# Column sums of squares in a two-block transformer kernel: from VectorE adds to accumulation in TensorE

## The chip, the cores and the metric

The kernel runs on one core of a Trainium2 chip. The metric is the device time of one execution in microseconds, the median of several runs. Inside the core, TensorE (PE) multiplies matrices and accumulates into PSUM, VectorE (DVE) and ScalarE (ACT) work element by element, GpSimd (POOL) does small jobs, and SyncE (SP) issues most of the DMA. Each engine runs its own queue in order, and the queues wait for each other on semaphores.

## What is computed

Two blocks on a sequence of 1024 tokens with 1024 features. The first has two layers, each an attention and a gated feed-forward network; the second is a mixer of a state-space model and short convolutions. Each stage begins with an RMS norm over the features:

```
def rmsnorm(x, g):
    y = x * lax.rsqrt(jnp.mean(x * x, axis=-1, keepdims=True) + RMS_EPS)
    return y * g

for i in range(DEPTH):                                   # first block, DEPTH = 2
    h = rmsnorm(x, norm_mix[i]) * (1 + sc1) + sh1        # norms 0 and 2
    x = x + g1 * attention_i(h)
    h = rmsnorm(x, norm_ffn[i]) * (1 + sc2) + sh2        # norms 1 and 3
    x = x + g2 * swiglu(h, ffn_w_in[i], ffn_w_out[i])
x = rmsnorm(x, final_norm)                               # folded with the next (4, 5)
... second block: rmsnorm, projections, scan, convolutions, out projection ...
return rmsnorm(h, final_norm_gain)                       # norm 6
```

The change concerns norms 1, 2, 3 and 6: norm 1 behind the first attention, norm 2 behind the first feed-forward stage, norm 3 behind the second attention, and norm 6 at the very end.

## The kernel before

The activations are held transposed: xT has 8 chunks (KC = 8) of 128 features on the partitions by 1024 tokens. A norm needs for each token the sum over all 1024 features. The kernel takes it in steps:

1. Each of the 8 chunks of the residual is finished by a VectorE add (L2337 behind attention, L2085 behind feed-forward, L2631 at the end). ScalarE squares it (L1565, at norm 6 L1900) into `squared(n, k)`.
2. VectorE adds the squares of chunks 1 to 7 into chunk 0 (`sum_squares`, L1966), one chunk behind the residual adds; the last add is in `deviations`.
3. TensorE multiplies the summed chunk by a column of ones (L1051): for each of 8 groups of 128 tokens the 128x128 square block is the stationary operand, and the moving operand has one column. The data are plain f32, and the trace has two instructions and two weight loads for each such matmul, so 16 of each for a chunk.
4. VectorE makes the variance (L1980), ScalarE its root (L1571), VectorE the reciprocal root (L1989 to L1993). TensorE spreads it over the partitions (L1059), and VectorE and ScalarE scale the chunks (L2022, L1579, L2018) for the next stage's matmuls. Norm 6 has no spread: TensorE transposes the result instead (L1541), and ScalarE and VectorE scale the transposed tiles (L1559, L2637) ahead of eight stores.

In TensorE's `norm(n)` the order is: 8 spare products into unused PSUM (L1044, they keep the engine working while it waits), the wait for the last VectorE sum, the narrow matmuls of step 3, 3 more spare products, the spread.

Behind the first feed-forward stage, TensorE makes the last down-projection in 8 tiles m = 0 to 7, six matmuls of 512 columns each (L1255). They go to four accumulators in PSUM in the order `LAST_PLACES = (2, 3, 0, 1, 2, 3, 2, 3)`; a tile whose place was used before waits until VectorE has added the earlier tile into xT (L2085). VectorE's loop there is `add_down(m)` and then `sum_squares(2, m - 1)`.

Which accumulator a step uses, and which counts of the semaphores it waits for, comes from a ledger (`plan_accumulators`), filled in program order.

Of the kernel before, what the change touches and what calls it, by code (L numbers as in the profile page):

```python
# [152 lines left out]
def plan_accumulators():  # L153
    use = Ledger()
    def norm(n):
        use.add(("norm sum", n), 3)
        use.add(("norm spread", n), 2, frees=0)

    for k in range(KC):
# [48 lines left out]
LAST_SPLITS = [name for name, _ in TILES if name[0] != "glu"]  # L208
MIX_TILES = [[(what, u) for u in us for what in ("kv", "q0", "q1")] for us in (range(4), range(4, 10))]
SPLITS = MIX_TILES[0] + [("wo", 0, m) for m in range(KC)] + MIX_TILES[1] + [("wo", 1, n) for n in range(4)] + LAST_SPLITS  # L210


def norm_turn(n):

    return min(n, 4) - 1
# [29 lines left out]
def two_blocks_kernel(nc, x, x_rows, c, ada_tiles, columns, ffn_w_in, ffn_w_out, a_tiles, a_w_out, a_sink,  # L245
# [6 lines left out]
    with ctx:  # L252
# [333 lines left out]
        def squared(n, k):  # L586

            return last_squares[k] if n == 6 else hT[:, k, :]
# [418 lines left out]
        def _(pe):  # L1007
# [38 lines left out]
            def norm(n):  # L1046
                dst, ready = take(("norm sum", n))
                spare_products(8, psum[:, 0:256] if n == 2 else psum[:, 3584:3840])
                pe.wait_ge(squares_summed, (KC - 1) * (norm_turn(n) + 1))
                for t in range(ST):  # L1050
                    mm = nc.tensor.matmul(dst[:, t:t + 1], squared(n, 0)[:, P * t:P * t + P], ones[:, :], start=True, stop=True)  # L1051
                mm.then_inc(ready, 1)
                if n == 6:
                    return
                dst, ready = take(("norm spread", n))
                spare_products(3)
                pe.wait_ge(rstd_ready, n + 1)
                for t in range(ST):
                    mm = nc.tensor.matmul(dst[:, P * t:P * t + P], rst[:, n, 4, t:t + 1].to_broadcast([P, P]), ident[:, :], start=True, stop=True)  # L1059
                mm.then_inc(ready, 1)  # L1060
                spare_products(8)
# [484 lines left out]
        def _(act):  # L1546
# [14 lines left out]
            def norm(n, wait_chunk, between=None):  # L1561
# [5 lines left out]
                        between(k)  # L1567
                if n == 2:
                    tile_highs(("q0", 4))
                act.wait_ge(acc_free[3], ACC[("norm sum", n)][2] + 1)  # L1570
                nc.scalar.activation(dev[:, n, :], var[:, n, :], ACT.Sqrt).then_inc(dev_ready, 1)  # L1571
                if n in (1, 3):
                    first_highs(n // 2)
# [337 lines left out]
        def _(dve):  # L1911
# [47 lines left out]

            def sum_squares(n, k):  # L1960

                if k > 0:
                    dve.wait_ge(squares, KC * norm_turn(n) + k + 1)
                    if (KC - 1) * norm_turn(n) + k > 1:
                        dve.wait_ge(squares_summed, (KC - 1) * norm_turn(n) + k - 1)
                    nc.vector.tensor_tensor(squared(n, 0), squared(n, 0), squared(n, k), ALU.add).then_inc(squares_summed, 1)  # L1966

            def norm(n):
# [6 lines left out]

            def deviations(n):

                sum_squares(n, KC - 1)
                a = ready(("norm sum", n))
                nc.vector.tensor_scalar(var[:, n, :], a[:, 0:ST], 1.0 / D, EPS, ALU.mult, ALU.add).then_inc(acc_free[3], 1)  # L1980
                dve.wait_ge(dev_ready, n + 1)
                reciprocal_root(n).then_inc(rstd_ready, 1)
                if n == 6:
                    dve.wait_ge(rstd_ready, 6)
# [53 lines left out]
            def feed(l, f):  # L2038
# [169 lines left out]
                for m in range(KC):  # L2208
                    add_down(STEPS - 1, m, acc[LAST_PLACES[m]])
                    if m == 0:  # L2210
                        down_lows(STEPS - 1, 1)
                    if l == 0:
                        sum_squares(2, m - 1)
                    if l == 1 and m == 1:
                        tile_lows(("conv", 0, 1))
                    if l == 1 and m >= 5:
                        gained_low(m - 5)
# [471 lines left out]
```

## Time and profile before

| | |
|---|---|
| median of 3 runs | 2823.31 us (2821.97 to 2825.81) |
| the profiled execution | 2823.84 us, span 2821.8 us |
| TensorE busy | 2692.6 us, 95% |
| VectorE busy | 1948.1 us, 69% |
| ScalarE busy | 1012.4 us, 36% |
| mean granted TensorE clock | 0.972 of full speed |

The span is from the first to the last instruction; the rest of the profiled execution's time lies around it. Busy shares are averages over stages. TensorE's clock has two levels, and the clock that the chip granted is given as a share of full speed: 1.00 is 2.4 GHz, 0.50 is 1.2 GHz. Weight loads (PEld) overlap with matmuls (PE).

### The profile page before, as it was taken

To read this page: it belongs to the slowest core of one execution; us is meant where nothing else is said; L and a number is where in the kernel's file an instruction comes from. 1 tells how busy PE (TensorE), PEld (TensorE's weight loads), DVE (VectorE), ACT (ScalarE), POOL (GpSimd) and SP (SyncE) were. 2 spreads that over 40 slices of the span, in tenths; PEclk is the share of its full clock that TensorE was granted. 3 is DMA by queue.
4 is the path that set the end of the run, shared out by engine and by line. 5 is a ranking of instruction groups with operands and counts; after the bars stand their busy time and mean duration, and the time that the engine had idled before them with its cause. 6 is when DMAs were issued, how large, how long until landed. Compare 5 with 4: busy or idle time off the path is not lost. (4 is left out here: it accounts for less than half of the span.)

```text
span 2821.8 us, 35472 instructions
## 1 busy us (share of the span) xinstructions
PE 2692.6 (95%) x12770; PEld 2120.5 (75%) x12770; DVE 1948.1 (69%) x3279; ACT 1012.4 (36%) x1789; POOL 271.9 (10%) x422
## 2 busy tenths in 40 slices
PE   6999699999999999999998989999999999999798
PEld 5666377788888888766675768888888878879767
DVE  6787747877778777667767597777777784331653
ACT  5554424333333332444444253333333341101232
POOL 2110000000000001101100000000000049920000
PEclk9999899999999999999998899999999999979899
DMA  5223321111111111223221111111111131121212
GB/s 225 98 98 101 138 90 53 49 52 50 55 51 52 56 48 49 97 68 98 91 82 75 34 38 57 51 56 52 48 56 52 49 113 38 45 46 32 82 38 75
DMA packets 172826, 193.08 MB, mean 68 GB/s; under 512 B 7952, under 2 KB 138224, under 8 KB 172432
## 3 DMA queue, kind: packets, MB, share of 16 engines
q1 hardware_dynamic: 160160, 147.45, 16.1%
q0 software_dynamic: 12560, 44.20, 5.1%
q8 instruction: 68, 1.11, 0.2%
q14 instruction: 38, 0.31, 0.0%
HBM read 177.86 MB, written 12.58 MB: 67 GB/s over the span
## 5 line engine op out<-in xcount | busy, mean ns | idle before, releaser
L2085 DVE SCALAR_TENSOR_TENSOR xT<-psum,mod,xT 128x1024 f32<-128x1024 f32 x352 | 446.6, 1280 | 143.0 <-PE psum L1255 143.0
L1255 PE MATMUL psum<-hT_high,w_low 128*128 128x512 f32 x1344 | 360.0, 390 | 4.1 <-DVE xT L2085 4.1
L1255 PEld LDWEIGHTS psum<-hT_high,w_low 128*128 128x128 f32 x1344 | 251.8, 188 | 58.6 <-DVE xT L2085 6.6
L1613 ACT ACTIVATE w_high<-wpair 128x512 fp32r<-128x512 f32 x294 | 184.6, 632 | 227.2 <-DMA wpair<-in_ffn_w_in_dram 129.4
L1036 PE MATMUL psum<-hT_high,w_low 128*128 128x512 f32 x944 | 260.2, 395 | 2.1 <-DVE arena L2481 2.1
L1036 PEld LDWEIGHTS psum<-hT_high,w_low 128*128 128x128 f32 x944 | 179.4, 191 | 40.5 <-DVE arena L2481 2.3
L1255 PE MATMUL psum<-h_low,w_low 128*128 128x512 f32 x672 | 207.6, 390 | 2.3 <-DVE h_low L2080 2.3
L1083 PE MATMUL psum<-hT_high,w_low 128*128 128x512 f32 x480 | 203.7, 424 | 1.9 <-DVE h_low_mix L2369 1.2
L1223 PE MATMUL psum<-hT_high,w_high 128*128 128x512 f32 x504 | 196.8, 391 | 3.5 <-DVE w_low L2045 3.5
L1732 ACT ACTIVATE arena<-arena 128x384 f32<-128x384 f32 (+3 forms) x320 | 157.7, 494 | 116.3 <-DVE arena L2266 116.3
L1224 PE MATMUL psum<-h_low,w_high 128*128 128x512 f32 x504 | 196.6, 390 | 0.0
L1225 PE MATMUL psum<-hT_high,w_low 128*128 128x512 f32 x504 | 196.4, 390 | 0.0
L1085 PE MATMUL psum<-hT_high,w_low 128*128 128x512 f32 x480 | 188.6, 393 | 0.0
L1084 PE MATMUL psum<-h_low_mix,w_low 128*128 128x512 f32 x480 | 187.8, 391 | 0.0
L2045 DVE TENSOR_TENSOR w_low<-wpair,w_high 128x512 fp32r<-128x512 f32 x252 | 172.8, 686 | 3.7
L2060 DVE TENSOR_TENSOR wpair<-wpair 128x512 f32<-128x512 f32 x168 | 115.9, 690 | 69.7 <-PE psum L1225 64.2
L1255 PEld LDWEIGHTS psum<-h_low,w_low 128*128 128x128 f32 x672 | 126.2, 188 | 29.2 <-DVE h_low L2080 3.1
L2351 DVE TENSOR_TENSOR w_low<-wpair,w_low 128x1024 fp32r<-128x1024 f32 x74 | 94.0, 1271 | 72.7 <-ACT w_low L1711 72.6
L1139 PE MATMUL psum<-arena 64*128 64x256 f32 (+3 forms) x640 | 119.8, 432 | 23.0 <-DVE arena L2260 20.8
L1083 PEld LDWEIGHTS psum<-hT_high,w_low 128*128 128x128 f32 x480 | 89.8, 187 | 64.0 <-issue 45.5
L1224 PE MATMUL psum<-hid_low,w_high 128*128 128x512 f32 x336 | 131.2, 391 | 0.0
L1631 ACT ACTIVATE hT<-hT 128x512 f32<-128x512 f32 x84 | 53.2, 633 | 168.3 <-DVE hT L2090 168.0
(340 smaller groups left out, 5261.1 us busy)
## 6 DMA issues: line engine op xcount, KB each, us to landing
wpair<-in_ffn_w_in_dram SPq DMA_DIRECT2D x176, 256.0 KB, 2.9
wpair<-in_ffn_w_out_dram SPq DMA_DIRECT2D x88, 256.0 KB, 2.8
wpair<-in_ada_tiles_dram POOLq DMA_DIRECT2D x20, 1024.0 KB, 5.4
wpair<-in_ada_tiles_dram POOLq DMA_DIRECT2D x32, 512.0 KB, 3.6
wpair<-in_w_in_dram SPq DMA_DIRECT2D x24, 512.0 KB, 3.8
wpair<-in_b_tiles_dram SPq DMA_DIRECT2D x18, 512.0 KB, 3.3
arena<-in_ada_tiles_dram SPq DMA_DIRECT2D x8, 1024.0 KB, 16.4
out_dram<-xT SPq DMA_DIRECT2D x16, 512.0 KB, 3.0
```

What stands on the lines that cost most here:

```text
L1036: mm = nc.tensor.matmul(dst[:, HALF * t:HALF * t + HALF], w(k), src(k)[:, HALF * t:HALF * t + HALF], start=first and n == 0 and w is high ...
L1083: nc.tensor.matmul(dst, high[:, k, :], hT_high[:, k, rows], start=k == 0, stop=False)
L1084: nc.tensor.matmul(dst, high[:, k, :], h_low_mix[:, k, rows], start=False, stop=False)
L1085: mm = nc.tensor.matmul(dst, low[:, k, :], hT_high[:, k, rows], start=False, stop=k == KC - 1)
L1223: nc.tensor.matmul(bank[dst], high[:, k, :], high_of(k), start=start and k == 0, stop=False, skip_group_check=not start)
L1224: nc.tensor.matmul(bank[dst], high[:, k, :], low_of(k), start=False, stop=False, skip_group_check=not start)
L1225: mm = nc.tensor.matmul(bank[dst], low[:, k, :], high_of(k), start=False, stop=k == 3, skip_group_check=not start)
L1255: mm = nc.tensor.matmul(dst[:, HALF * t:HALF * t + HALF], w, src[:, t, :], start=n == 0, stop=n == 2)
L1613: nc.scalar.activation(part_high[name], part_raw[name], ACT.Copy).then_inc(part_high_ready, 1)
L1732: e = nc.scalar.activation(s, s, ACT.Exp, bias=stat_n[:, ti, h:h + 1], accum_out=stat_l[:, ti, h:h + 1])
L2045: nc.vector.tensor_tensor(part_low[name], part_raw[name], as_f32(part_high[name]), ALU.subtract).then_inc(part_split, 1)
L2085: nc.vector.scalar_tensor_tensor(xT[:, m, :], acc[m % 2] if src is None else src, mod[:, l, 40 + m:41 + m], xT[:, m, :], ALU.mult, ALU.add ...
```

## The change

At norms 1, 3 and 6 VectorE still adds chunks 0 to 5, and TensorE accumulates this sum and the squares of chunks 6 and 7 as three series of narrow matmuls into the same eight PSUM columns. At norm 2 VectorE adds nothing; TensorE accumulates all eight chunks. The sum of norm 2 goes to accumulator 1 instead of 3, so it waits for the add of tile 3.

```
 def plan_accumulators():
     use = Ledger()
     def norm(n):
-        use.add(("norm sum", n), 3)
+        use.add(("norm sum", n), 1 if n == 2 else 3)
...
+SUMMED_ALONE = {1: (6, 7), 2: tuple(range(1, KC)), 3: (6, 7), 6: (6, 7)}
+SUMS = KC - 3
+
+def sums_before(n):
+    return SUMS * {1: 0, 2: 1, 3: 1, 6: 2}[n]
...
             def norm(n):                                       # TensorE
                 dst, ready = take(("norm sum", n))
                 spare_products(8, psum[:, 0:256] if n == 2 else psum[:, 3584:3840])
-                pe.wait_ge(squares_summed, (KC - 1) * (norm_turn(n) + 1))
-                for t in range(ST):
-                    mm = nc.tensor.matmul(dst[:, t:t + 1], squared(n, 0)[:, P * t:P * t + P], ones[:, :], start=True, stop=True)
+                if n != 2:
+                    pe.wait_ge(squares_summed, sums_before(n) + SUMS)
+                else:
+                    pe.wait_ge(down_added, KC * (STEPS - 1) + 4)
+                for k in (0,) + SUMMED_ALONE[n]:
+                    if k or n == 2:
+                        pe.wait_ge(squares, KC * norm_turn(n) + k + 1)
+                    for t in range(ST):
+                        mm = nc.tensor.matmul(dst[:, t:t + 1], squared(n, k)[:, P * t:P * t + P], ones[:, :], start=k == 0 and t == 0,
+                                              stop=k == KC - 1, skip_group_check=True)
                 mm.then_inc(ready, 1)
...
             def sum_squares(n, k):                             # VectorE
-                if k > 0:
+                if 0 < k <= SUMS:
                     dve.wait_ge(squares, KC * norm_turn(n) + k + 1)
-                    if (KC - 1) * norm_turn(n) + k > 1:
-                        dve.wait_ge(squares_summed, (KC - 1) * norm_turn(n) + k - 1)
+                    if sums_before(n) + k > 1:
+                        dve.wait_ge(squares_summed, sums_before(n) + k - 1)
...
             def deviations(n):
-                sum_squares(n, KC - 1)
...
                     add_down(STEPS - 1, m, acc[LAST_PLACES[m]])
                     if m == 0:
                         down_lows(STEPS - 1, 1)
-                    if l == 0:
-                        sum_squares(2, m - 1)
```

How this stands in the queues: first TensorE's queue behind the first feed-forward stage, before the change. The first rows are the down-projection's last tile, then the spare products, the sum of squares, spare products and the spread (x8 counts the program's matmuls, each two instructions in the trace).

```order
L1255 MATMUL psum<-w_high,w_low 128x512 x4
L1255 MATMUL psum<-hid_high,w_low 128x512 x2
L1044 MATMUL psum<-pick,ident 128x256 x8
L1051 MATMUL psum<-ones,hT 128x1 x8
L1044 MATMUL psum<-pick,ident 128x256 x3
L1059 MATMUL psum<-ident,rst 128x128 x8
```

And the same place of TensorE's queue after the change, with the changed kernel's line numbers.

```order
L1271 MATMUL psum<-w_high,w_low 128x512 x4
L1271 MATMUL psum<-hid_high,w_low 128x512 x2
L1053 MATMUL psum<-pick,ident 128x256 x8
L1066 MATMUL psum<-ones,hT 128x1 x64
L1053 MATMUL psum<-pick,ident 128x256 x3
L1075 MATMUL psum<-ident,rst 128x128 x8
```

Nothing moved; the narrow matmuls are 64 instead of 8. At norms 1, 3 and 6 they are 24 instead of 8 in the same way.

VectorE's queue at this place before the change: the weights' low part for tiles 4 to 7 (L2075), the adds of tiles 1 and 2, then sums of squares between the adds, and the variance.

```order
L2075 TENSOR_TENSOR w_low<-wpair,w_low 128x512
L2085 SCALAR_TENSOR_TENSOR xT<-psum,mod,xT 128x1024 x2
L1966 TENSOR_TENSOR hT<-hT 128x1024
L2085 SCALAR_TENSOR_TENSOR xT<-psum,mod,xT 128x1024
L1966 TENSOR_TENSOR hT<-hT 128x1024
L2085 SCALAR_TENSOR_TENSOR xT<-psum,mod,xT 128x1024
```

VectorE's queue after the change, from the same instruction to the reciprocal root.

```order
L2090 TENSOR_TENSOR w_low<-wpair,w_low 128x512
L2100 SCALAR_TENSOR_TENSOR xT<-psum,mod,xT 128x1024 x7
L1995 TENSOR_SCALAR var<-psum 128x8
L2004 RECIPROCAL rst<-dev 128x8
L2005 TENSOR_TENSOR rst<-rst 128x8
```

The adds of tiles 1 to 7 now stand directly behind each other.

## Rows read from the trace of the kernel before

**Rows 1.** The page: busy time of each engine, its share, instructions.

```profile
PE 2692.6 (95%) x12770; PEld 2120.5 (75%) x12770; DVE 1948.1 (69%) x3279; ACT 1012.4 (36%) x1789; POOL 271.9 (10%) x422
```

**Rows 2.** The chain that ended last, its end (start us, us, what).

```profile
2803.72 1.23 DVE arena L1966
...
2805.00 1.95 PE psum L1051 x16
```

**Rows 3.** Timeline at norm 1 (start us, us, engine, line [idle before]).

```profile
443.61 3.44 PEld L1044 LDWEIGHTS psum<-pick,ident 128*128 128x128 f32 x16
...
445.24 2.54 DVE L1966 TENSOR_TENSOR hT<-hT 128x1024 f32<-128x1024 f32 x2
445.36 1.06 ACT L1565 ACTIVATE hT<-xT 128x1024 f32<-128x1024 f32 x1 [9.81 <-DVE xT L2337]
...
447.84 1.86 PEld L1051 LDWEIGHTS psum<-ones,hT 128*128 128x128 f32 x16 [0.79 <-DVE hT L1966]
...
449.62 1.17 PEld L1044 LDWEIGHTS psum<-pick,ident 128*128 128x128 f32 x6
...
454.48 3.32 PEld L1044 LDWEIGHTS psum<-pick,ident 128*128 128x128 f32 x16
```

**Rows 4.** Timeline behind the first feed-forward stage and at norm 2.

```profile
1124.44 0.87 PEld L1255 LDWEIGHTS psum<-w_high,w_low 128*128 128x128 f32 x4
...
1125.80 0.87 PEld L1255 LDWEIGHTS psum<-w_high,w_low 128*128 128x128 f32 x4
...
1128.53 2.46 DVE L2085 SCALAR_TENSOR_TENSOR xT<-psum,mod,xT 128x1024 f32<-128x1024 f32 x2
...
1130.93 1.23 DVE L1966 TENSOR_TENSOR hT<-hT 128x1024 f32<-128x1024 f32 x1
...
1135.73 0.76 PEld L1255 LDWEIGHTS psum<-w_high,w_low 128*128 128x128 f32 x4 [4.48 <-DVE xT L2085]
...
1140.34 3.44 PEld L1044 LDWEIGHTS psum<-pick,ident 128*128 128x128 f32 x16
...
1145.17 1.86 PEld L1051 LDWEIGHTS psum<-ones,hT 128*128 128x128 f32 x16 [1.39 <-DVE hT L1966]
...
1146.95 2.08 PEld L1044 LDWEIGHTS psum<-pick,ident 128*128 128x128 f32 x6
```

**Rows 5.** Timeline at norm 3, TensorE's weight loads.

```profile
1605.46 3.44 PEld L1044 LDWEIGHTS psum<-pick,ident 128*128 128x128 f32 x16
...
1609.68 2.00 PEld L1051 LDWEIGHTS psum<-ones,hT 128*128 128x128 f32 x16 [0.79 <-DVE hT L1966]
1611.56 2.26 PEld L1044 LDWEIGHTS psum<-pick,ident 128*128 128x128 f32 x6
```

**Rows 6.** Timeline at norm 6.

```profile
2800.30 3.44 PEld L1044 LDWEIGHTS psum<-pick,ident 128*128 128x128 f32 x16
...
2802.05 1.07 ACT L1900 ACTIVATE arena<-xT 128x1024 f32<-128x1024 f32 x1 [8.43 <-DVE xT L2631]
...
2806.70 7.06 PEld L1541 LDWEIGHTS psum<-ident,arena 128*128 128x128 f32 x64
```

**Rows 7.** Stretches: length, busy by engine (instructions), granted clock, DMA share, GB/s.

```profile
450.50:451.00 0.50, 0.50 (x4) 0.26 (x2) 0.43 (x3) 0.50 (x2) 0.00 (x0) 0.82 0.00 0
...
454.00:454.50 0.50, 0.50 (x6) 0.50 (x5) 0.00 (x0) 0.00 (x0) 0.00 (x0) 0.77 0.98 285
...
1147.00:1147.50 0.50, 0.50 (x4) 0.41 (x4) 0.17 (x1) 0.15 (x1) 0.00 (x0) 0.64 0.00 0
...
1609.70:1611.30 1.60, 1.60 (x15) 1.60 (x15) 0.00 (x0) 0.00 (x0) 0.00 (x0) 1.00 0.00 0
...
1611.30:1611.40 0.10, 0.10 (x2) 0.10 (x3) 0.00 (x0) 0.00 (x0) 0.00 (x0) 0.74 0.00 0
...
2810.80:2820.00 9.20, 3.19 (x30) 2.95 (x28) 3.59 (x3) 2.23 (x2) 0.00 (x0) 0.80 1.02 405
```

**Rows 8.** Last weight load of norm 3's series, by itself.

```profile
1611.35 0.33 PEld L1051 LDWEIGHTS psum<-ones,hT 128*128 128x128 f32 x1
```

More of the change, by code:

```diff
@@ L1569, in norm @@
                     tile_highs(("q0", 4))
-                act.wait_ge(acc_free[3], ACC[("norm sum", n)][2] + 1)
+                act.wait_ge(acc_free[ACC[("norm sum", n)][0]], ACC[("norm sum", n)][2] + 1)
                 nc.scalar.activation(dev[:, n, :], var[:, n, :], ACT.Sqrt).then_inc(dev_ready, 1)
@@ L1976, in deviations @@
             def deviations(n):
-                sum_squares(n, KC - 1)
                 a = ready(("norm sum", n))
-                nc.vector.tensor_scalar(var[:, n, :], a[:, 0:ST], 1.0 / D, EPS, ALU.mult, ALU.add).then_inc(acc_free[3], 1)
+                nc.vector.tensor_scalar(var[:, n, :], a[:, 0:ST], 1.0 / D, EPS, ALU.mult, ALU.add).then_inc(free(("norm sum", n)), 1)
                 dve.wait_ge(dev_ready, n + 1)
```

## The prediction

> **What bounds the kernel now.** The page comes first [rows 1]: TensorE is busy 95% of the span and VectorE 69%. So this is a kernel whose time is TensorE's queue plus the places where that queue waits. The chain that ended last, at its end [rows 2], shows what such a place looks like: a VectorE add of squares (L1966), then the norm's sixteen narrow matmul instructions (L1051), and behind them the output's transposes [rows 6]. A norm is therefore serial, and whatever lengthens it lengthens the kernel, unless something else was late anyway.
>
> The timeline around the four norms tells who is late [rows 3 to 6]. At each of them TensorE first issues eight spare products (sixteen weight loads in the trace, 3.44 us). It is done with those at 447.05 at norm 1, then stands until 447.84, because the sum of the squares is not ready: two VectorE adds in a row (2.54 us from 445.24) follow the last residual add. The wait for VectorE is 0.79 us at norm 1, the same at norm 3 (1608.90 to 1609.68), 1.26 at norm 6, 1.39 at norm 2. That is all that the wait is worth, since 3.44 us of it is already filled with spare products. ScalarE's last square (445.36 and 1.06 us) ends at 446.42, before the spare products do.
>
> Norm 2 has a second wait, ahead of these. TensorE's down-projection tiles 6 and 7 reuse accumulators that VectorE must have added first, and between these adds VectorE sums squares: 4.48 us before 1135.73 [rows 4].
>
> **The change, part by part.** *Removed from VectorE:* two adds at norms 1, 3 and 6, all seven at norm 2. *Added to TensorE:* a series of 8 narrow matmuls (sixteen instructions of one column, each with a 128-column weight load) for each chunk no longer added: 2 at norms 1, 3 and 6, 7 at norm 2, so 13 series in all. They stand behind the spare products in TensorE's queue and in front of the variance, so everything in the norm waits for them.
>
> *Price of a series at the full clock.* Sixteen weight loads from 2805.00 until the next group's at 2806.70 are 1.70 us, 0.106 each [rows 2, 6]; at norms 1 and 2 the group takes 1.78, the 0.08 over it being the change to the next kind of instruction, counted once. Three series are then 5.18 us and eight 13.68 (5.10 at norm 6, read from its own row).
>
> *Norms 1, 3 and 6, full clock.* All squares but the last are early, and the last is there at 446.42, so the series starts as the spare products end: 447.05 + 5.18 = 452.23 where the next group started at 449.62 before: +2.6. Norm 3: 1608.90 + 5.18 = 1614.08 against 1611.56, +2.5. Norm 6: spare products end at 2800.30 + 3.44 = 2803.74 (the last square, 2802.05 and 1.07, is ready by then), + 5.10 = 2808.84 against 2806.70, +2.1.
>
> *Norm 2, full clock.* First the gain. With no sums between, VectorE's adds follow each other as the two at 1128.53 do, 1.19 apart: the add of tile 3 starts at 1130.93, that of tile 4 at 1132.12, and it ends at 1133.40. TensorE goes on there instead of at 1135.73. A tile is 1.36 us (1124.44 to 1125.80); tile 7 needs the add of tile 5, which ends at 1134.59, before tile 6 is through at 1134.76. So tile 7 is through at 1136.12 instead of 1140.34: 4.2 us gained. The spare products end at 1139.56; tile 7's last matmul (0.4 behind its load), add (1.28) and square (1.06) are over at 1138.9, so nothing is waited for. Then eight series: 1139.56 + 13.68 = 1153.24 against 1146.95, +6.3. The chunks 0 to 5 that TensorE could take during its wait are not taken there, since they stand behind tile 7.
>
> The sum at the full clock is 2.6 + 6.3 + 2.5 + 2.1 = 13.5 us more. Every stage behind a norm starts from its result, and the profile shows no other late partner there (TensorE's 128-column spread, VectorE's and ScalarE's scaling and the first products follow each other), so I let all of it through. The stores of x and the second layer's tiles start up to 5 us earlier at norm 2; nobody waits for them.
>
> *What the clock adds.* In three of the four norms the granted clock fell to 0.5 (1.2 of 2.4 GHz) around the narrow series, while TensorE issued without a gap or nearly so [rows 7]: at 450.8, 1147.2 and 1611.35. Counted from the end of the spare products' loads, that is 3.8, 3.4 and 2.4 us. From 1609.7 to 1611.3 the row has TensorE and its weight loads busy 1.60 of 1.60 us, all of it narrow, and the clock falls right behind it; at norm 1 more than a microsecond of spare products behind the series did not prevent the fall. At norm 6 it held, with 128-column transposes from 2806.7 on. I conclude that narrow matmuls hardly hold the clock. Once it is down a pair takes twice as long: the last load of the series starts at 1611.35, the next group's first at 1611.56, 0.21 instead of 0.106 [rows 5, 8].
>
> The rule to weigh against this is in the Trainium skill, "TensorE: Matmul & The Clock Gate", Part 1: a monitor sets the clock by how busy TensorE has been, and idleness lets it fall. A gapless series would by that rule keep 2.4 GHz, and the sum would stay at 13.5. The row at 1609.7 to 1611.3 speaks against it. The same page, under LDWEIGHTS, puts a load at its columns divided by 1.2 in ns, 107 for 128 columns; the trace agrees at full clock (0.106) and not behind the fall (0.21), and by the page's figure the sum would again be 13.5.
>
> So I let the clock fall 3.8 us into each new series and stay down while only narrow matmuls run. I take the longest of the three because the three short series could show no later fall; the shortest, 2.4, and a later one, 5.5 (half as much again as the longest), are the bounds. Norm 1: 3.8 + 2 x 1.38 = 6.56, ends 453.61, +4.0. Norm 3: +3.9. Norm 6: 3.8 + 2 x 1.30 = 6.4, ends 2810.14, +3.4. Norm 2: 3.8 + 2 x 9.88 = 23.56, ends 1163.12 against 1146.95, +16.2. Behind norm 6 the transposes then start at the low clock; the eight stores move 405 GB/s from 2810.8 to the end and so leave the transposes several microseconds of room, but the first tile comes later: 0.5, between 0 and 1.0. Behind the others the spare products and the spread already met the low clock for part of their way (449.62 to 454.48, 4.86 us, at norm 1 [rows 3]; at the low clock throughout it would be 2.26 for six loads [rows 5] and 3.4 for 16 pairs at 0.21, 5.7): 0.5 each, between 0 and 0.9.
>
> **Sum:** 4.0 + 16.2 + 3.9 + 3.4 + 0.5 + 1.5 = 29.5 us. The profiled execution took 2823.84 us (span 2821.8), 0.5 over the median of 2823.31, so the sum goes on the median: 2852.8. Bounds: with the fall at 2.4 us 5.4 + 17.6 + 5.3 + 4.8 + 1.0 + 2.7 = 36.8, with it at 5.5 and nothing behind 2.6 + 14.5 + 2.5 + 2.1 = 21.7; this case alone spans 2845 to 2860.
>
> **The rivals.**
> *The clock holds* through the narrow series: 13.5 us, 2836.8. For it: norm 6, where it held over 1.7 us. Against it: the three others. 10%. It is what the Trainium skill's rule of "TensorE: Matmul & The Clock Gate", Part 1, would have for a gapless series.
> *The clock falls and comes back inside norm 2's long series*, as it came back at 454.2 after 450.8 at norm 1 [rows 7]. There, however, wide products ran. Norm 2 would then have two low stretches of 3.4 us, each losing 1.7: 13.5 + 3.4, and 1.4 + 1.4 + 1.3 at the other norms, + 2.0 behind: 23.0, 2846.3. 10%.
> *The added series cost nothing, VectorE's relief does.* Then only the waits go: 0.79 + 0.78 + 1.26, and 1145.17 - 1139.56 = 5.6 at norm 2, together 8.4 us faster, 2814.9. It decides at 8.4 / 13 = 0.65 us for a series, where the trace has 1.70 for the very same instructions, and nothing runs in parallel with them. 2%, with another 2% for about no change.
> *The likeliest*, clock down for most of norm 2's series: 76%.
>
> **The numbers.** Predicted 2852.8. The range is 2836 to 2860: it takes in the two milder cases and the likeliest up to its upper bound. About 0.2% of the time, 5.6 us, is what a measurement tells from no change. All cases but the last rival lie above it: slower 0.95, same 0.03, faster 0.02.
>
> **What would show it.** In the profile after: sixteen-fold groups of narrow loads x48 at norms 1, 3 and 6 and x128 at norm 2, starting the moment the spare products end, with no wait for VectorE; TensorE's wait at the down-projection's tile 6 about 2 us instead of 4.48; the norm 2 series some 22 to 25 us long, with a granted clock of 0.5 over most of it. If that series is 13.7 us long at 1.00, the first rival is right; if the clock alternates in it, the second. I am wrong altogether if the norms' variance comes no later than before.

## The result, and the profile after

The changed kernel takes 2854.34 us in the median of 4 runs (2853.91 to 2855.61), the kernel before 2822.64 beside it on the same chip (4 runs, 2821.88 to 2825.81). The ratio is 1.0111 with a 95% interval of 1.0093 to 1.0128: slower by 31.7 us. 2852.8 was predicted. The profiled execution took 2855.61 us, its span is 2853.2 us, 31.4 more than before.

The page of the changed kernel, to set against [rows 1]: busy time, share of the span, instructions.

```profile
PE 2729.2 (96%) x12978; PEld 2161.0 (76%) x12978; DVE 1931.6 (68%) x3266; ACT 1012.6 (35%) x1789; POOL 270.1 (9%) x422
```

TensorE has 208 instructions more, 13 series of 16, and is busy 36.6 us longer; VectorE has 13 fewer and is busy 16.5 us less. Series for add, the two look like an even exchange. The time went to the engine that had none to spare.

Timeline of the changed kernel's TensorE weight loads at norm 1 and at norm 2 (start us, us, engine, line, operands, count, [idle before, whom it waited for]); L1066 are the narrow matmuls, L1053 the spare products, L1075 the spread, L1271 the down-projection.

```profile
444.27 3.44 PEld L1053 LDWEIGHTS psum<-pick,ident 128*128 128x128 f32 x16
447.73 6.87 PEld L1066 LDWEIGHTS psum<-ones,hT 128*128 128x128 f32 x48
454.48 2.25 PEld L1053 LDWEIGHTS psum<-pick,ident 128*128 128x128 f32 x6
...
1138.68 0.77 PEld L1271 LDWEIGHTS psum<-w_high,w_low 128*128 128x128 f32 x4 [2.20 <-DVE xT L2100]
...
1141.32 3.44 PEld L1053 LDWEIGHTS psum<-pick,ident 128*128 128x128 f32 x16
1144.78 24.60 PEld L1066 LDWEIGHTS psum<-ones,hT 128*128 128x128 f32 x128
1169.26 2.25 PEld L1053 LDWEIGHTS psum<-pick,ident 128*128 128x128 f32 x6
```

The waits in front of the series [rows 3, 4, 5, 6] are gone, the one at tile 6 has shrunk from 4.48 to 2.20 us, and in their place stands one row of 24.60 us. Its 128 loads would take 13.7 us at the 0.106 us of [rows 2, 6]. Windows of the same stretch say why it is longer (length, busy time and instructions of PE, PEld, DVE, ACT, POOL, granted clock, DMA share, GB/s).

```profile
1144.80:1148.00 3.20, 3.20 (x30) 3.17 (x28) 0.00 (x0) 1.54 (x2) 0.00 (x0) 1.00 0.63 220
1148.00:1149.00 1.00, 1.00 (x7) 1.00 (x7) 0.00 (x0) 0.00 (x0) 0.00 (x0) 0.54 0.00 0
1149.00:1169.00 20.00, 20.00 (x95) 20.00 (x95) 0.00 (x0) 0.00 (x0) 0.00 (x0) 0.50 0.00 1
```

The third window has TensorE busy 20.00 of 20.00 us at a granted clock of 0.50 (1.2 GHz): 95 instructions, 0.21 us each, where 28 loads in 3.2 us were 0.114 at full clock. PE's busy share hides this entirely: an engine at half speed reads as 100%.

The same timeline at norm 3 and at norm 6 (L1557 are the transposes of the output).

```profile
1627.88 3.44 PEld L1053 LDWEIGHTS psum<-pick,ident 128*128 128x128 f32 x16
1631.34 6.13 PEld L1066 LDWEIGHTS psum<-ones,hT 128*128 128x128 f32 x48
1637.36 2.25 PEld L1053 LDWEIGHTS psum<-pick,ident 128*128 128x128 f32 x6
...
2828.51 3.44 PEld L1053 LDWEIGHTS psum<-pick,ident 128*128 128x128 f32 x16
2831.97 5.54 PEld L1066 LDWEIGHTS psum<-ones,arena 128*128 128x128 f32 x48
2837.35 8.72 PEld L1557 LDWEIGHTS psum<-ident,arena 128*128 128x128 f32 x64
```

Where the 31.4 us of the span are, measured in both traces from the first spare product of a norm to what follows the spread (at norm 6 to the first transpose, and from there to the end):

| place | predicted | measured |
|---|---|---|
| norm 1, series and spread | 4.0 + 0.5 | 15.31 - 10.87 = 4.4 |
| norm 2, down-projection relieved | -4.2 | -4.3 |
| norm 2, series and spread | 20.4 + 0.5 | 33.91 - 11.36 = 22.5 |
| norm 3, series and spread | 3.9 + 0.5 | 15.31 - 10.76 = 4.6 |
| norm 6, series and transposes | 3.4 + 0.5 | 2.4 + 0.8 |
| stages that the change doesn't touch | 0 | 1.0 |

The last row is of the size of the scatter. Its largest pieces are +1.2 us from norm 3's end to norm 6 and -1.1 us from norm 2's end to norm 3. With the same instructions, the twelve traces told of below and these two lie between 1183.3 and 1188.6 us on the first way and between 452.5 and 454.5 us on the second.

### The profile page after: what moved, and what is told of

It is laid out like the page before. It is cut to its first block and busy times, and to the rows that moved or that the text cites. A ratio compares the mean times of both kernels' runs of the same rounds, so it can differ in the third digit from the quotient of the medians.

```text
span 2853.2 us, 35863 instructions
## 1 busy us (share of the span) xinstructions
PE 2729.2 (96%) x12978; PEld 2161.0 (76%) x12978; DVE 1931.6 (68%) x3266; ACT 1012.6 (35%) x1789; POOL 270.1 (9%) x422
## 5 line engine op out<-in xcount | busy, mean ns | idle before, releaser
L1271 PE MATMUL psum<-hT_high,w_low 128*128 128x512 f32 x1344 | 360.0, 390 | 4.1 <-DVE xT L2100 4.1
L1271 PEld LDWEIGHTS psum<-hT_high,w_low 128*128 128x128 f32 x1344 | 251.9, 188 | 58.6 <-DVE xT L2100 6.6
L1271 PE MATMUL psum<-h_low,w_low 128*128 128x512 f32 x672 | 207.6, 390 | 2.3 <-DVE h_low L2095 2.3
L2075 DVE TENSOR_TENSOR wpair<-wpair 128x512 f32<-128x512 f32 x168 | 115.8, 689 | 70.0 <-PE psum L1241 64.2
L1271 PEld LDWEIGHTS psum<-h_low,w_low 128*128 128x128 f32 x672 | 126.2, 188 | 29.2 <-DVE h_low L2095 3.1
L1239 PEld LDWEIGHTS psum<-hT_high,w_high 128*128 128x128 f32 x504 | 95.0, 188 | 24.3 <-DVE w_low L2060 4.6
## 6 DMA issues: line engine op xcount, KB each, us to landing
arena<-in_ada_tiles_dram SPq DMA_DIRECT2D x8, 1024.0 KB, 16.5
```

Source lines behind the costliest of these rows:

```text
L1239: nc.tensor.matmul(bank[dst], high[:, k, :], high_of(k), start=start and k == 0, stop=False, skip_group_check=not start)
L1271: mm = nc.tensor.matmul(dst[:, HALF * t:HALF * t + HALF], w, src[:, t, :], start=n == 0, stop=n == 2)
```

## The experiments

None of the kernels leaves out work. Edits are against the changed kernel; `ADDED_SUMS` are the chunks that VectorE still adds, `SUMMED_ALONE` those that TensorE accumulates. Line numbers are each kernel's own, `...` marks a cut, and a switch that has one value in a kernel is written as that value.

| kernel | median us | before beside it | ratio, 95% interval |
|---|---|---|---|
| n136_only | 2838.23 | 2825.24 | 1.0048 (1.0027 to 1.0069) |
| n2_only | 2841.38 | 2825.24 | 1.0054 (1.0037 to 1.0071) |
| moving128 | 2834.66 | 2824.65 | 1.0039 (1.0024 to 1.0055) |
| before_moving128 | 2822.35 | 2824.65 | 0.9995 (0.9986 to 1.0004) |
| split_moving128 | 2825.84 | 2824.65 | 1.0003 (0.9994 to 1.0012) |
| early_two | 2823.22 | 2824.65 | 0.9996 (0.9987 to 1.0005) |
| split_late_wait | 2819.26 | 2824.39 | 0.9979 (0.9970 to 0.9988) |
| n136_m128_no_lead | 2819.62 | 2824.39 | 0.9980 (0.9970 to 0.9990) |

Four more had one run each and are read by their traces: wide_between 2867.52, twice_narrow 2890.21, wide_every_two 2860.56, no_spares2 2851.88.

### Are the parts additive?

```diff
+SUMMED_ALONE = {1: (6, 7), 2: (), 3: (6, 7), 6: (6, 7)}                    # n136_only
+SUMMED_ALONE = {1: (), 2: (1, 2, 3, 4, 5, 6, 7), 3: (), 6: ()}             # n2_only
```

> The change at norms 1, 3 and 6 alone; norm 2 as before. Theory (each extra series of narrow matmuls costs 1.70 us at the full clock and 3.4 once the clock has fallen, 2.4 to 5.6 us into the series, and the spread behind it runs slowly too): the three shares of the change's trace, 4.6 + 5.8 + 3.2 = 13.6 us over before, 11 to 16. Rival (narrow matmuls at the full clock only): 7.2 us. Rival (the shares of the norms are not additive, norm 2 carries all): under 5 us.

> The change at norm 2 alone. Theory: VectorE's relief lets the down-projection end 4.3 us earlier, the eight series take 24 to 25 us (3 to 5 us at the full clock, the rest at half) instead of a wait and one series: 17 us over before, 15 to 19. With the clock held: 6.3 us. If VectorE's relief were worth nothing: 21 us.

Measured: +13.0 and +16.1 us by the medians, both as expected, and 29.1 together against 31.7 for both at once. The intervals are some 5 us wide for each part. So neither part is a gain, and nothing beyond this noise says that they act on each other. (The share of 5.8 us that is given for norm 3 holds 1.2 us of the stage behind it, which the change doesn't touch; norm 3 alone is 4.6 in the table above.)

### Is it the clock, and what makes it fall?

`ks` is the list of chunks of a norm. Three kernels put other work into norm 2's series: a spare product of 256 columns behind every fourth narrow matmul (wide_between), another 64 narrow matmuls into unused PSUM behind the series (twice_narrow), and a spare product behind every second (wide_every_two). A fourth has none of the eight spare products ahead of the series (no_spares2).

```diff
                     for t in range(ST):
                         mm = nc.tensor.matmul(dst[:, t:t + 1], squared(n, k)[:, P * t:P * t + P], ones[:, :],
                                              start=k == ks[0] and t == 0 and not (n == 2 and EARLY), stop=k == ks[-1], skip_group_check=True)
+                        if n == 2 and t % HOLD == HOLD - 1 and not (k == ks[-1] and t == ST - 1):    # HOLD = 4, 2
+                            spare_products(1, psum[:, 512:768])
...
+                if n == 2:                                                                          # twice_narrow
+                    for k in range(8):
+                        for t in range(ST):
+                            mm = nc.tensor.matmul(psum[:, 512 + t:513 + t], squared(n, k)[:, P * t:P * t + P], ones[:, :], start=True, stop=True)
...
+                spare_products(0 if n == 2 else 8, psum[:, 512:768] if n == 2 else psum[:, 3584:3840])   # no_spares2
```

> The changed kernel with one spare product (256 columns, 0.43 us) behind every fourth narrow matmul at norm 2, 15 more spare products in all. Theory (the fall of the clock makes the series slow): if the spare products hold the clock, the narrow pairs stay at 0.106 us and the whole series takes 13.7 + 6.5 = 20.2 us, 4 us less than in the changed kernel, though TensorE has more to do. If every fourth is too seldom, the clock falls and the series takes 31 to 37 us. Rival (narrow matmuls that accumulate on one another are slow by themselves, whatever the clock): 24.5 + 6.5 = 31 us with the clock at 1.00.

> The changed kernel with eight more series of narrow matmuls at norm 2, each into a PSUM column of its own without accumulation, and the variance waiting for them. Theory (once the clock is down, narrow matmuls never bring it back, and a series costs 16 x 0.213 = 3.4 us): 27.2 us over the changed kernel, the granted clock 0.50 through the whole of it. Rival (the clock recovers now and then): 14 to 22 us. Rival (only accumulation on the same column is slow): the added half at 0.106 a pair, 13.6 us.

> The changed kernel with one spare product of 256 moving columns behind every second narrow matmul of norm 2's series (31 more than in wide_between's place without any). Theory (the clock falls because one-column matmuls give the array too little to do): the clock holds at 1.00, a narrow matmul takes 0.106 us, a spare product 0.43 us here, so the series takes 13.7 + 13.4 = 27 us at clock 1.00. Rival (31 wide products are still too few): the clock falls as in wide_between and the series takes over 40 us. Rival (narrow matmuls are slow by themselves after some number of them): 35 to 38 us at clock 1.00.

> The changed kernel without the eight spare products that stand ahead of norm 2's series, so that the series starts right behind tile 7's product. Theory: the fall of the clock is set by the series itself, it comes 2.5 to 5 us into it, the series takes 24 to 25 us, and the stretch is 3.4 us shorter than in the changed kernel. Rival (the spare products are what holds the clock up for the first microseconds): the fall comes under 2 us into the series, which takes 25.5 us or more, and the stretch is at most 2 us shorter.

TensorE's weight loads in wide_between, early and later in its series: the same eight loads (four narrow matmuls) take 1.08 us, and 2.04 once the clock is down.

```profile
1144.93 1.08 PEld L1070 LDWEIGHTS psum<-ones,hT 128*128 128x128 f32 x8
...
1148.69 2.04 PEld L1070 LDWEIGHTS psum<-ones,hT 128*128 128x128 f32 x8
```

One wide product in five was too little: the clock fell all the same, and the series took 36.5 us, within the 31 to 37 expected for that case. In wide_every_two it is one in three, and the clock held. The first and last narrow pair of that series, and the window over all of it:

```profile
1144.49 0.63 PEld L1070 LDWEIGHTS psum<-ones,hT 128*128 128x128 f32 x4
...
1171.72 0.63 PEld L1070 LDWEIGHTS psum<-ones,hT 128*128 128x128 f32 x4
1172.27 1.17 PEld L1056 LDWEIGHTS psum<-pick,ident 128*128 128x128 f32 x6
```

```profile
1144.50:1172.20 27.70, 27.70 (x192) 26.08 (x190) 0.00 (x0) 1.55 (x2) 0.00 (x0) 1.00 0.08 27
```

27.8 us where 27 was expected. A full 31 wide products are added to 64 narrow ones, and the stretch is only 3.3 us longer than the 24.5 of the changed kernel. The narrow matmuls themselves run at full speed to the last, so it isn't their number, their weight loads or the accumulation into one bank that slows them.

twice_narrow shows the other side: the clock does not come back as long as nothing but narrow matmuls runs.

```profile
1145.14 23.98 PEld L1070 LDWEIGHTS psum<-ones,hT 128*128 128x128 f32 x128
1169.00 27.43 PEld L1077 LDWEIGHTS psum<-ones,hT 128*128 128x128 f32 x128
```

The second 128 loads take 27.3 us, 0.213 each. The kernel's one run is 35.9 us over the changed kernel, where 27.2 were expected. The stretch at norm 2 is 25.8 us longer: the added 27.3, less 1.5 by which the first half of the series and the spread are shorter. Norm 3 is 1.6 and norm 6 2.7 us longer, since the clock fell earlier in their series, and the rest is in stages that the edit doesn't touch.

In no_spares2 the series starts directly behind the down-projection's last tile.

```profile
1141.10 24.71 PEld L1070 LDWEIGHTS psum<-ones,hT 128*128 128x128 f32 x128
1165.69 2.25 PEld L1056 LDWEIGHTS psum<-pick,ident 128*128 128x128 f32 x6
```

```profile
1143.00:1144.00 1.00, 1.00 (x11) 1.00 (x10) 0.00 (x0) 1.00 (x2) 0.00 (x0) 1.00 0.89 344
1144.00:1145.00 1.00, 1.00 (x8) 1.00 (x8) 0.00 (x0) 0.98 (x2) 0.00 (x0) 0.66 1.12 381
1145.00:1165.00 20.00, 20.00 (x95) 20.00 (x95) 0.00 (x0) 1.14 (x1) 0.00 (x0) 0.50 0.08 29
```

The fall comes 3.2 us into the series (the window to 1145 has 0.66: a third of it at the high level), the series takes 24.6 us, and the stretch is 3.4 us shorter (30.54 against 33.91). The spare products neither held the clock nor hastened its fall; ahead of a series that waits for nothing they were pure cost.

### The same instructions with more columns

The column of ones is broadcast to 128 moving columns: the same number of matmuls and weight loads, 128 equal result columns, of which VectorE reads one.

```diff
-                        mm = nc.tensor.matmul(dst[:, t:t + 1], squared(n, k)[:, P * t:P * t + P], ones[:, :],
-                                              start=k == ks[0] and t == 0, stop=k == ks[-1], skip_group_check=True)
+                        mm = nc.tensor.matmul(dst[:, P * t:P * t + P], squared(n, k)[:, P * t:P * t + P], ones[:, 0:1].to_broadcast([P, P]),
+                                              start=k == ks[0] and t % 4 == 0, stop=k == ks[-1], skip_group_check=True)
```

> The changed kernel with the ones as a moving operand of 128 columns instead of one, so each narrow matmul writes 128 equal columns and the variance reads one of them; the number of matmuls, weight loads and waits is that of the changed kernel. Theory (narrow matmuls are bound by their weight load, and let the clock fall since they put hardly a column through the array): a pair takes 0.110 us as the output's transposes do, the clock stays at 1.00, the series at norm 2 takes 14.2 us instead of 24.5, those at the other norms 5.3, and the spreads behind them lose no time: 13 to 17 us less than the changed kernel, some 2838. Rival (accumulation on the same place is slow by itself): the series stays at 24 us or more. Rival (the load and not the columns decides the clock): the clock falls as before, and the series takes 24 to 25 us.

```profile
1141.60 14.48 PEld L1070 LDWEIGHTS psum<-ones,hT 128*128 128x128 f32 x128
1155.99 1.17 PEld L1056 LDWEIGHTS psum<-pick,ident 128*128 128x128 f32 x6
```

```profile
1141.00:1155.30 14.30, 14.30 (x126) 14.20 (x125) 0.00 (x0) 2.16 (x2) 0.00 (x0) 1.00 0.20 68
```

A hundred and twenty-eight times the arithmetic, and norm 2's series takes 14.4 us instead of 24.5. The clock stays at 1.00. With 2834.66 us the kernel is some 20 us under the changed one, more than the 13 to 17 expected. The series came out as expected; what was reckoned too small is the spreads, which are 6.1 us shorter together than the changed kernel's (3.60, 3.60 and 3.59 us, with the three spare products, against 5.10, 5.97 and 5.83), and 3.5 us shorter than those of the kernel before. This kernel is still 10.0 us over the one before: by the same segments as in the table above +1.7 at norm 1, -4.4 + 10.1 at norm 2, +1.8 at norm 3 and +2.5 at norm 6, 11.7 us.

The same edit on the kernel before, with nothing moved to TensorE:

```diff
+SUMMED_ALONE = {1: (), 2: (), 3: (), 6: ()}
```

> The kernel before, sums of squares all on VectorE, with the ones as 128 moving columns. Theory: the clock no longer falls at norms 1, 2 and 3, the three spare products and the spread take 3.7 us instead of 4.7 to 4.9, the series 1.76 instead of 1.70: 2 to 4 us less than before. Rival (the wait ahead of the series lets the clock fall as well): no difference beyond 1 us.

Norms 1 to 3 are shorter by 1.3, 1.3 and 1.2 us (9.60, 10.02 and 9.60). The median is 2.3 us under the kernel before, but the interval goes from 4.0 us less to 1.1 us more, so the times are in line with the theory (2 to 4 us less) and with the rival (no difference) alike. Two things in the traces bear on it. What is won at norm 1 is lost again 50 us later: the way from norm 1's end to norm 2's end is 697.5 us against 697.2, though norm 2 itself is shorter. In both kernels TensorE stands idle for some 2.4 us ahead of the next feed-forward products (from 503.88 in the kernel before, from 502.21 here). Behind this wait the clock stays at 1.00 in the kernel before and falls to half here, and of 1.7 us of lead 0.2 are left 4.4 us later. Windows, the kernel before first:

```profile
502.00:506.00 4.00, 2.12 (x9) 1.80 (x10) 4.00 (x4) 1.52 (x1) 0.00 (x0) 1.00 0.00 0
```

```profile
502.00:506.00 4.00, 3.79 (x10) 3.09 (x11) 4.00 (x4) 0.00 (x0) 0.00 (x0) 0.57 0.00 0
```

And whether the clock falls behind a single narrow series at all differs between executions: at norm 1 early_two has the very instructions of the kernel before, one series of one column, and there the clock did not fall (1.00 from 444.0 to 450.5) and the segment took 9.50 us instead of 10.87.

With both kernels of 128 columns side by side, the price of moving the sums is read without the low clock at the norms: 2834.66 against 2822.35, 12.3 us by the medians.

### Can TensorE take a part of the sums where it waits?

split_moving128 uses 128 columns, takes chunks 6 and 7 at norms 1, 3 and 6 with no spare products ahead, and at norm 2 has VectorE add chunks 4 to 6, while TensorE takes chunk 1 in its wait ahead of tile 6 and chunks 2, 3 and 7 behind tile 7. early_two keeps one column and the other norms as before, and takes chunks 1 and 2 in the wait.

```diff
+SUMMED_ALONE = {1: (6, 7), 2: (1, 2, 3, 7), 3: (6, 7), 6: (6, 7)}      # split; early_two: 2: (1, 2), else ()
...
+                        if l == 0 and places is LAST_PLACES and m == 6:
+                            sums, _ = take(("norm sum", 2))
+                            pe.wait_ge(down_added, KC * (STEPS - 1) + 3)
+                            for k in EARLY:                             # (1,); early_two: (1, 2), and one column as in the changed kernel
+                                pe.wait_ge(squares, KC * norm_turn(2) + k + 1)
+                                for t in range(ST):
+                                    nc.tensor.matmul(sums[:, P * t:P * t + P], squared(2, k)[:, P * t:P * t + P], ones[:, 0:1].to_broadcast([P, P]),
+                                                     start=k == EARLY[0] and t % 4 == 0, stop=False, skip_group_check=True)
```

> A version meant to beat both: 128 moving columns; no spare products ahead of a norm's sum, since the series itself holds the clock; at norms 1, 3 and 6 chunks 6 and 7 alone as in the change; at norm 2 chunk 1 while TensorE waits ahead of the down-projection's tile 6, chunks 2, 3 and 7 behind tile 7, and VectorE adds chunks 4 to 6. Theory: the norms end 0.7 (1 and 3), 1.1 (6) and 2.8 us (2) earlier than before, and 1 us at each of norms 1 to 3 comes from the clock: 6 to 9 us less than before. Rival (each added series is on the path whatever the clock): norms 1, 3 and 6 slower by 2 us each, so 0 to 3 us more than before.

> The kernel before with one thing changed at norm 2: TensorE takes the squares of chunks 1 and 2 as narrow series (one moving column) while it waits ahead of tile 6, and VectorE adds the other five. Theory (a series costs nothing where TensorE waits, and two VectorE adds fewer shorten the chain behind tile 7 by 2.3 us; the clock is down there in the kernel before as well): 1.5 to 3 us less than before. Rival (narrow matmuls keep the clock down longer than idling did): no difference or 1 us more.

Both came out at no change: split_moving128 at 1.2 us over the kernel before, where 6 to 9 less were expected, and early_two at 1.4 us less, with an interval from 3.7 less to 1.4 more that holds theory and rival. In split_moving128 the norms 1, 3 and 6 gained 1.8, 1.7 and 0.9 us (9.07, 9.08 and 5.47 us), about what was expected (1.7, 1.7 and 1.1). Norm 2 lost 1.2 us from tile 4 to the spread's end. These segments sum to 3.2 us of gain; in this trace it is eaten up by 1.6 us ahead of norm 1, 1.6 between norm 1 and tile 4 (the clock is down at 504 as in before_moving128) and 3.9 behind norm 3. Norm 2's row shows 4.47 us idle in front of all the series: the wait for VectorE's last sum, which only chunk 0 needs, stood at the head. The row of the matmuls themselves, the last of the three, names VectorE's add as what ended it. Behind this idle time the clock was low for a while as well: the 64 loads take 8.77 us, 7.2 at moving128's rate.

```profile
1132.61 1.98 PEld L1277 LDWEIGHTS psum<-ones,hT 128*128 128x128 f32 x16
...
1141.82 8.85 PEld L1070 LDWEIGHTS psum<-ones,hT 128*128 128x128 f32 x64 [4.47 <-issue]
1141.85 9.01 PE L1070 MATMUL psum<-ones,hT 128*128 128x128 f32 x64 [4.08 <-DVE hT L2001]
```

In early_two two narrow series fill TensorE's wait, and the clock falls behind them, so that the down-projection's tiles, which the wait had held up before, are now slow instead: from 1131.5 to 1134.0 the granted clock is 0.54. From tile 4 to the spread's end norm 2 takes 21.78 us against 23.05 before, 1.3 less.

```profile
1127.77 3.77 PEld L1277 LDWEIGHTS psum<-ones,hT 128*128 128x128 f32 x32
```

```profile
1131.50:1134.00 2.50, 2.50 (x9) 1.91 (x8) 1.82 (x2) 1.06 (x1) 0.20 (x1) 0.54 0.70 283
```

The last two kernels follow from this: split_late_wait puts chunks 2 and 3 ahead of the wait for VectorE's sum, then chunk 0 and 7. n136_m128_no_lead leaves norm 2 as before but for the 128 columns.

```diff
+                ks = ks[1:-1] + (0, ks[-1])                            # split_late_wait, norm 2
                 for k in ks:
+                    if k == 0 and n == 2:
+                        pe.wait_ge(squares_summed, sums_before(n) + len(ADDED_SUMS[n]))
...
+SUMMED_ALONE = {1: (6, 7), 2: (), 3: (6, 7), 6: (6, 7)}                # n136_m128_no_lead
+                spare_products(8 if n == 2 else 0, psum[:, 0:256] if n == 2 else psum[:, 3584:3840])
```

> The kernel of split_moving128 with TensorE's order at norm 2 changed: the series of chunks 2 and 3, which wait for squares only, stand ahead of the wait for VectorE's last sum, then chunk 0 (which carries that sum), then chunk 7. Theory (the 4.47 us that TensorE stood idle in split_moving128 is VectorE's sum arriving late in front of series that do not need it): norm 2's series end some 4 to 5 us earlier than in split_moving128, norms 1, 3 and 6 stay at their gains there (-1.8, -1.7, -0.9 us), and the whole is 6 to 9 us under the kernel before, 0.2 to 0.3%, ratio 0.997 to 0.998. Rival (VectorE is late by more once TensorE reads the squares): TensorE waits as long, in front of chunk 0, and the whole is within 2 us of split_moving128, ratio 1.000.

> Column sums with 128 moving columns; norms 1, 3 and 6: chunks 6 and 7 on TensorE, without the spare products ahead of them; norm 2 as in the kernel before, VectorE sums all and one series follows. Theory (an added series costs 1.7 us only where TensorE had nothing to wait for; at these norms it stands in the wait that the spare products filled): norm 1 -1.8, norm 3 -1.7, norm 6 -0.9 and norm 2 -1.3 us, together -5.7 us, ratio 0.998. Rival (the added series is on the path wherever it stands): 0 to +3 us, ratio 1.000 to 1.001.

split_late_wait, norm 1 and norm 2 (L1074 are the series, L1281 the early one):

```profile
443.81 5.55 PEld L1074 LDWEIGHTS psum<-ones,hT 128*128 128x128 f32 x48
...
452.88 3.32 PEld L1056 LDWEIGHTS psum<-pick,ident 128*128 128x128 f32 x16
...
1131.23 1.98 PEld L1281 LDWEIGHTS psum<-ones,hT 128*128 128x128 f32 x16
...
1135.98 3.76 PEld L1074 LDWEIGHTS psum<-ones,hT 128*128 128x128 f32 x32
1140.35 3.65 PEld L1074 LDWEIGHTS psum<-ones,hT 128*128 128x128 f32 x32 [0.61 <-DVE hT L2005]
1143.92 1.17 PEld L1056 LDWEIGHTS psum<-pick,ident 128*128 128x128 f32 x6
```

The wait of 4.47 us is 0.61. From tile 4 to the spread's end norm 2 takes 18.94 us, 5.3 less than in split_moving128 and 4.1 less than before. The kernel is faster than the one before by 5.1 us in the median, 0.2% (interval 0.1 to 0.3), a little under the 6 to 9 us expected. In this trace the segments add up to 8.5 us of gain; 1.5 of it are lost between norm 1's end and tile 4, where the granted clock from 502 to 506 is 0.57 as in before_moving128, and the untouched stage behind norm 3 was 4.0 us longer, as it was in split_moving128's. Whether that last part is scatter or something this order brings about stays open.

n136_m128_no_lead gains 4.8 us where 5.7 was expected: norms 1, 3 and 6 as expected (9.07, 9.07, 5.47), norm 2's segment -1.4, and 1.7 us more between norm 1 and norm 2, 1.5 of it ahead of tile 4 (the clock at 502 again, 0.57) and 0.3 in tiles 6 and 7.

Not all of this gain comes from the moved sums. At norm 1, before_moving128, which moves nothing, has 9.60 us of the way from 10.87 to 9.07, and early_two, where the clock happened to hold, 9.50. So some 1.3 us are the clock and 0.5 the move, and at norm 3 nearly the same (10.76, 9.60, 9.07). At norm 6 all of the 0.9 is the move. The sums moved at these norms are thus worth about 2 us in all, by the segments; no run takes them apart by its time. Nor does the time show what split_late_wait moves at norm 2: from tile 4 to the spread's end it takes 3.0 us less than n136_m128_no_lead (18.94 against 21.89), and the medians are 0.4 us apart.

Windows over tiles 6 and 7, this kernel's first, then that of the kernel before, which [rows 4] don't show:

```profile
1135.00:1136.00 1.00, 0.33 (x1) 0.33 (x2) 1.00 (x2) 0.35 (x1) 0.92 (x2) 0.50 0.42 168
1136.00:1138.00 2.00, 2.00 (x6) 1.50 (x6) 2.00 (x3) 0.73 (x2) 0.07 (x1) 0.50 0.65 262
1138.00:1140.00 2.00, 2.00 (x6) 1.61 (x5) 2.00 (x2) 1.04 (x1) 0.00 (x0) 0.50 0.61 250
```

```profile
1136.00:1138.00 2.00, 1.70 (x6) 0.79 (x5) 2.00 (x3) 0.77 (x1) 0.12 (x1) 0.72 0.65 262
1138.00:1140.30 2.30, 2.25 (x5) 1.82 (x6) 2.30 (x3) 1.06 (x1) 0.00 (x0) 0.50 0.56 228
```

Around TensorE's wait of 4.45 us the clock is down too, in the kernel before from about 1137 on, and tiles 6 and 7 run at half speed for part of their way.

## Why the prediction was right

- *TensorE is what the kernel waits for at the norms.* Right: what was added to its queue there went into the time, and VectorE's 16.5 us less did not come out of it, except at tiles 6 and 7 and in the waits of 0.79 to 1.39 us ahead of the series, which the sum had counted.
- *13.5 us at full clock.* moving128 measures this term, the clock aside: 11.7 us by the segments, 10.0 by the medians. Its series were 0.3 to 0.7 us longer than priced (0.112 a load), which makes 15.1; against that the spreads at norms 1 to 3 are 1.1 to 1.3 us shorter each than before when the clock holds, -3.5, since the kernel before had the low clock there. Against before_moving128, which has the high clock there too, the term is 12.3 us by the medians.
- *4.2 us of relief at tiles 6 and 7.* Right in size (4.3), with one part that I had not named. The wait ahead of tile 6 shrank by 2.28 us. From tile 6's start to the spare products it is 4.61 us before and 2.64 after, 2.0 less: 1.08 of it is a second wait, for the add of tile 5 ahead of tile 7, which is gone as predicted, and 0.9 is tile 7 itself, 2.29 us at the low clock before and 1.37 after, when the clock held. The sum had it in, because it priced both tiles at 1.36 us without asking at which clock they ran. Tile 7's row before, then after:

```profile
1138.05 1.35 PEld L1255 LDWEIGHTS psum<-w_high,w_low 128*128 128x128 f32 x4 [1.08 <-DVE xT L2085]
```

```profile
1139.95 0.87 PEld L1271 LDWEIGHTS psum<-w_high,w_low 128*128 128x128 f32 x4
```

- *The clock falls 3.8 us into a series and stays down.* Right at norms 1, 2 and 3, where it fell 4.0, 3.3 and 4.9 us in, within the bounds of 2.4 to 5.5 (the upper one is called half as much again as 3.8, which would be 5.7). At norm 6 this step was wrong: the clock held to the end of the series (5.38 us) and fell in the transposes, 5.7 us after the series began. The series took 6.75, 24.48, 6.02 and 5.38 us against 6.56, 23.56, 6.56 and 6.4. The exact 3.8 was in part luck: in the traces with three one-column series at a norm, such a group took from 5.38 to 8.06 us (norm 6 of the changed kernel and of twice_narrow), so the moment of the fall differs by some microseconds from one execution to the next.
- *Afterwards.* The three spreads cost 0.2, 1.2 and 1.2 us, 2.6 together, where 1.5 stood in the sum; norm 6's transposes and stores 0.8 instead of 0.5.
- *The size.* 29.5 us were predicted and 31.7 measured. By the table above, norm 2 with its spread was 1.6 us over its terms, norm 6 0.7 under, and 1.0 lies in untouched stages.
- *The rivals.* "The clock holds" and "it falls and comes back" are refuted by one row, 20.00 us at 0.50, and twice_narrow extends it to 27.3 us more. "The added series cost nothing" is refuted by n136_only.

By the rule of the Trainium skill, "TensorE: Matmul & The Clock Gate", Part 1, that the monitor follows how busy TensorE is and idleness lowers the clock, the series should have kept 2.4 GHz. No run here bears that out for one-column matmuls: TensorE, never idle in the series, lost its clock in every series of 64 of them and in every group of 24 at norms 1 and 3. At norm 6 it lost it in one group of six and within half a microsecond behind the five others. In moving128, where each instruction has 128 columns, it kept the clock in all of them.

Where my expectations failed is in the second half. In split_moving128 the wait for VectorE's sum stood ahead of series that didn't need it, and only the trace showed that. And a gain at norm 1 was taken to reach the end whole, where 1.5 us of it were lost again when the clock fell at 502.

## What to carry to other kernels

A reduction by one-column matmuls is priced by its weight loads (0.106 us for 128 columns here) and, once it goes on for more than some microseconds, by the clock that it loses (0.213): give such a series wide moving operands, even useless columns, or mix wide products in. Work moved from VectorE to the engine that is busy 95% paid only where that engine stood waiting, and by little: some 2 us at norms 1, 3 and 6, with every wait as late in its queue as the data allow. Spare products belong ahead of a wait; where the wait goes, they have to go too. A gain of a microsecond or two has to be followed to the end of the kernel, since the clock may fall elsewhere and take it back.

## What the runs showed of the hardware

- Busy share did not hold the clock: 20.00 of 20.00 us busy at a granted clock of 0.50. More columns did: at the same instruction count 128 columns kept 1.00 through 14.3 us, and so did one product of 256 columns for every two narrow matmuls; one for every four did not. What it is in the wider products that holds the clock, no run takes apart.
- 128 columns of plain f32 cost as good as nothing over one column at full clock: 14.4 us for 128 instructions, 0.112 each, against 0.106. The matmuls overlap with the weight loads: in moving128's window of 14.30 us the one is busy for 14.30 us and the other for 14.20.
- A weight load of 128 columns takes 0.106 us at the high level and 0.213 at the low. The second is twice_narrow's, 27.3 us for 128. The Trainium skill ("TensorE: Matmul & The Clock Gate", LDWEIGHTS) puts a load at its columns divided by 1.2 in ns, which is 107 for 128 columns. The traces agree at the high level and not at the low.
- A wait can cost more than its idle time. Around the waits of 4.5 us ahead of tile 6 the clock fell, and tile 7 took 2.29 us in the kernel before and 2.54 in n136_m128_no_lead, against 1.37 in the changed kernel: some 1 us more.
- The same wait need not have the same effect. Behind some 2.4 us of idle time at 502 the clock stayed at 1.00 in the kernel before and fell to half in before_moving128, at a cost of 1.5 us. The fall behind one narrow series at norm 1 came in the kernel before (10.87 us) and not in early_two (9.50). What decides it is not shown.
